# Modulation parts in four pieces, two PE sums moved into blocks, and a gate vector made as rows

## The reference, cut to what matters

```python
mod = split(silu(c) @ ada_w + ada_b, 6)              # six vectors of 1024
a = rmsnorm(x, g_pre) * (1 + mod[1]) + mod[0]
y = short_gated_conv(a)                              # a @ w_in (1024x3072), conv of 3 taps, @ w_out
h = x + mod[2] * rmsnorm(y, g_post)                  # mod[2]: the first gate vector
f = square(relu((rmsnorm(h, g_pre_ff) * (1 + mod[4]) + mod[3]) @ mlp_w_in)) @ mlp_w_out
h = h + mod[5] * rmsnorm(f, g_post_ff)
```

## Time and profile before

| | us |
|---|---|
| median of 3 runs | 749.37 (749.32 to 749.52) |
| profiled execution | 749.81 |
| its span, first to last instruction | 747.8 |
| PE busy | 740.4 (99%) |
| PEld, DVE, ACT, POOL busy | 690.1, 551.4, 366.7, 12.2 |
| granted TensorE clock | 1.00 in the whole span |
| bytes read from HBM | 151 MB, mean 203 GB/s |

### The profile page before, as it was taken

The page is one execution under the profiler, slowest core; times in us unless marked ns, Lnnn a source line. Parts: engine busy times, 40 slices in busy tenths (PEclk is TensorE's granted clock), DMA queues, the critical chain, the costliest instruction groups (busy, mean ns, idle before and its releaser), DMA issues.

```text
span 747.8 us, 13266 instructions
## 1 busy us (share of the span) xinstructions
PE 740.4 (99%) x5368; PEld 690.1 (92%) x5368; DVE 551.4 (74%) x767; ACT 366.7 (49%) x455; POOL 12.2 (2%) x29
## 2 busy tenths in 40 slices
PE   8999999999999999999999999999999999999998
PEld 8889956999998888899979999999999999999998
DVE  4569888865556734499899967859879988887441
ACT  4145232745553333496555366585556655554330
POOL 0000000000000000020000011000000000000000
PEclk9999999999999999999999999999999999999999
DMA  9999997354566967536545342437554555443640
GB/s 312 349 368 360 393 351 298 125 215 169 176 205 209 341 194 252 169 128 226 174 166 185 105 160 99 137 128 261 187 204 142 198 202 191 151 146 121 208 136 29
DMA packets 53583, 152.70 MB, mean 204 GB/s; under 512 B 2912, under 2 KB 34016, under 8 KB 43296
## 3 DMA queue, kind: packets, MB, share of 16 engines
q1 hardware_dynamic: 52704, 149.43, 58.3%
q0 software_dynamic: 544, 1.84, 0.7%
q10 hardware_dynamic: 288, 0.76, 0.3%
HBM read 150.97 MB, written 1.05 MB: 203 GB/s over the span
## 4 chain that ended last, share of the span: by engine, by line
PE 84%; DVE 8%; SPq 3%; ACT 3%; issue 1%; DMA 1%; DVEq 0%; ACTq 0%
PE ps L1533 19%; PE ps L1534 19%; PE ps L1535 19%; PE ps L1712 4%; PE ps L1713 4%; PE ps L1711 4%; PE ps L1758 4%; DVE w_lo L934 3%; SPq L420 2%; DVE cacc L1307 2%; PE ps L1617 1%; ACT w_hi L561 1%; DMA raw<-in_ada 1%; PE ps L1882 1%; PE ps L1880 1%
## 5 line engine op out<-in xcount | busy, mean ns | idle before, releaser
L934 DVE TENSOR_TENSOR w_lo<-raw,w_hi 128x2048 fp32r<-128x2048 f32 (+2 forms) x116 | 246.0, 2124 | 83.1 <-ACT w_hi L561 83.1
L1533 PE MATMUL ps<-a_hi,w_hi 128*128 128x256 f32 x1024 | 290.2, 283 | 0.0
L1534 PE MATMUL ps<-a_lo,w_hi 128*128 128x256 f32 x1024 | 289.0, 282 | 0.0
L1535 PE MATMUL ps<-a_hi,w_lo 128*128 128x256 f32 x1024 | 288.6, 282 | 0.0
L561 ACT ACTIVATE w_hi<-raw 128x2048 fp32r<-128x2048 f32 (+2 forms) x116 | 205.8, 1778 | 97.8 <-PE ps L1713 43.9
L1533 PEld LDWEIGHTS ps<-a_hi,w_hi 128*128 128x128 f32 x1024 | 193.2, 189 | 1.2 <-issue 0.7
L1534 PEld LDWEIGHTS ps<-a_lo,w_hi 128*128 128x128 f32 x1024 | 192.5, 188 | 0.6 <-issue 0.5
L1535 PEld LDWEIGHTS ps<-a_hi,w_lo 128*128 128x128 f32 x1024 | 192.8, 188 | 0.0
L1533 PE MATMUL ps<-up_hi,w_hi 128*128 128x256 f32 x192 | 54.7, 285 | 0.0
L1534 PE MATMUL ps<-up_lo,w_hi 128*128 128x256 f32 x192 | 54.2, 282 | 0.0
L1535 PE MATMUL ps<-up_hi,w_lo 128*128 128x256 f32 x192 | 53.8, 280 | 0.0
(11 more groups left out here) (289 smaller groups left out, 949.3 us busy)
## 6 DMA issues: line engine op xcount, KB each, us to landing
raw<-in_w_z_in SPq DMA_DIRECT2D x26, 1024.0 KB, 4.8
raw<-in_w_up SPq DMA_DIRECT2D x22, 1024.0 KB, 4.8
raw<-in_w_mlp_in SPq DMA_DIRECT2D x16, 1024.0 KB, 5.0
raw<-in_w_mlp_out SPq DMA_DIRECT2D x16, 1024.0 KB, 6.1
raw<-in_w_down SPq DMA_DIRECT2D x16, 704.0 KB, 4.1
raw<-in_ada_half SPq DMA_DIRECT2D x8, 1024.0 KB, 6.8
raw<-in_ada SPq DMA_DIRECT2D x8, 1024.0 KB, 6.5
raw<-in_w_sc_in SPq DMA_DIRECT2D x8, 768.0 KB, 7.1
```

The lines of the kernel that those rows point to most:

```text
L934: e.tensor_tensor(w_lo[:, slot, 0:words], raw[:, unit_slot, 0:words], w_hi[:, slot, 0:words].bitcast(f32), SUB).then_inc(raw_used, 1)
L1533: e.matmul(dst, w_hi[:, slot, cols], hi, start=start, stop=False, skip_group_check=skip)
L1534: e.matmul(dst, w_hi[:, slot, cols], lo, start=False, stop=False, skip_group_check=skip)
L1535: return e.matmul(dst, w_lo[:, slot, cols], hi, start=False, stop=stop, skip_group_check=skip)
```

## The change

1. Each part is loaded in four pieces in place of three, all of 256 KB (`PIECES`). DVE and PE wait for them piece by piece; the order of their operations stays. `COLUMNS_BEHIND` for tile 1 goes from product 9 to product 8.
2. `mod_sums` for vector 2, `widen`, the bias sum and weight product in columns, and the two copies are gone. In their place PE makes two products of 512 columns with a stationary matrix of ones (`row_sums`), which leave the sum over partitions as a row on every partition. They stand in group (0, 1) behind its fourth product. DVE adds the bias row and multiplies by the weight row (`gain_rows`), and does so between the low parts of mlp_in blocks 0 and 1.
3. The two rows come over DRAM: once PE is through the split keys, POOL writes columns of `par` (norm weight, bias) as rows to `param_rows` and reads each back on all partitions into `y`.
4. The sum for the convolution's mean moves behind the second product of the next block, the folded sum of ln2 behind the first k of the first up block.

```diff
-PIECES = [(0, 0, 4), (1, 0, 2), (1, 2, 4)]
+PIECES = [(0, 0, 2), (0, 2, 4), (1, 0, 2), (1, 2, 4)]
...
+            e.wait_ge(w_used, USED)
+            e.wait_ge(act_hi, DT)
+            e.wait_ge(act_lo, DT)
+            for n, (name, first) in enumerate((("gains", 8), ("ada_b", 16))):
+                e.dma_start(param_rows[n:n + 1, :].rearrange("o (i p) -> p (o i)", p=P), pcol(name, first, DT),
+                            allow_slow_non_contiguous=True).then_inc(row_out, 16)
+            e.wait_ge(row_out, 32)
+            for n in range(2):
+                e.dma_start(flat(y[:, 4 * n:4 * n + 4, :]), param_rows[n:n + 1, :].broadcast_to([P, D])).then_inc(row_in, 16)
...
-            def gain_evict(dst, n):
-
+            def gain_rows(dst):
+
+                e.wait_ge(row_in, 32)
+                start = ch.n
                 for h in range(2):
-                    e.wait_ge(gain_wide, 2 * n + h + 1)
-                    e.tensor_copy(dst[:, h * 512:(h + 1) * 512], ps[:, 6 + h, :]).then_inc(gain_in, 1)
-                e.wait_ge(gain_in, 2 * n + 2)
+                    cols = slice(h * 512, (h + 1) * 512)
+                    e.wait_ge(gain_wide, h + 1)
+                    ch.mark(e.tensor_tensor(dst[:, cols], ps[:, 6 + h, :], flat(y[:, 4 + 2 * h:6 + 2 * h, :]), ADD))
+                for h in range(2):
+                    cols = slice(h * 512, (h + 1) * 512)
+                    ch.wait(start + h + 1)
+                    e.tensor_tensor(dst[:, cols], dst[:, cols], flat(y[:, 2 * h:2 * h + 2, :]), MUL).then_inc(gain_in, 1)
...
             ahead_at(g0)
+            gain_rows(gain_b)
             ahead_at(g0 + 1)
-            mods(0, 2)
-            e.tensor_tensor(gain_post[:, :], mod[:, 16:24], pcol("gains", 8, 8), MUL).then_inc(gain_cols, 1)
...
-            COLUMNS_BEHIND = {1: 9, 3: 8, 5: 6}
+            COLUMNS_BEHIND = {1: 8, 3: 8, 5: 6}
...
+            def row_sums(acc):
+
+                for h in range(2):
+                    e.matmul(ps[:, 6 + h, :], ones[:, :], acc[:, h * 512:(h + 1) * 512], start=True, stop=True).then_inc(gain_wide, 1)
...
-                        if (c, h) == (1, 0) and k == 4:
-                            widen(gain_post, 0)
+                        if (c, h) == (0, 1) and k == 4:
+                            e.wait_ge(raw_used, ring_unit("half", 7) + 1)
+                            row_sums(ada_acc[:, 0, :])
...
-                    if (c, h) == (0, 1):
-                        e.wait_ge(raw_used, ring_unit("half", 7) + 1)
-                        mod_sums(2, ada_acc[:, 0, :], MISC)
...
+                    elif s == CV_MEAN_STEP + 1:
+                        pair_block(raw_unit(g0 + s) + 1, g0 + s, f % 2, a_hi, a_lo, lambda t: conv_mean() if t == 1 else None)
...
+                    if k == 1:
+                        folded_pairs_sum()
```

More of the change, by code:

```diff
@@ L255, in build_program @@
         x_new = sem("x_new")
-        part_in = [[sem(f"part_in{i}_{h}") for h in range(3)] for i in range(PARTS)]
+        part_in = [[sem(f"part_in{i}_{h}") for h in range(len(PIECES))] for i in range(PARTS)]
         key_in = [[sem(f"key_in{q}_{h}") for h in range(2)] for q in range(4)]
@@ L275, in build_program @@
         gain_wide = sem("gain_wide")
+        row_out = sem("row_out")
+        row_in = sem("row_in")
+        param_rows = nc.dram_tensor("param_rows", (2, D), f32).ap()
         gain_row_out = sem("gain_row_out")
@@ L430, in pair_parts @@
                     for u in both:
-                        for piece in range(3):
+                        for piece in range(len(PIECES)):
                             part_piece(u, piece)
                 else:
-                    for piece in range(3):
+                    for piece in range(len(PIECES)):
                         for u in both:
@@ L509, in _ @@
             constant(e.memset(sc_cv[:, :, :], 0.0), 4)
-            e.wait_ge(gain_cols, 2)
+            e.wait_ge(w_used, USED)
[7 more added lines that the diff above has]
+                e.dma_start(flat(y[:, 4 * n:4 * n + 4, :]), param_rows[n:n + 1, :].broadcast_to([P, D])).then_inc(row_in, 16)
+            e.wait_ge(gain_cols, 1)
             e.dma_start(gain_row.rearrange("o (i p) -> p (o i)", p=P), gain_post_ff[:, :],
@@ L1080, in token_chain @@
                 behind()
-            MOD_SUMMED, MOD_BANK = (1, 2, 3, 4), (MISC, 0, 1, MISC)
+            MOD_BANK = (0, 1, MISC)
             def mods(number, vector):
-                e.wait_ge(mod_ps, MOD_SUMMED[number])
+                e.wait_ge(mod_ps, number + 1)
                 cols = slice(8 * vector, 8 * vector + 8)
@@ L1215, in _ @@
             ahead_at(g0)
+            gain_rows(gain_b)
             ahead_at(g0 + 1)
-            mods(0, 2)
-            e.tensor_tensor(gain_post[:, :], mod[:, 16:24], pcol("gains", 8, 8), MUL).then_inc(gain_cols, 1)
             for i in range(2):
                 ada_unit(ring_unit("shift", i), 2 * i, ada_acc[:, 2, :])
-            gain_evict(gain_b, 0)
+            e.wait_ge(gain_in, 2)
             e.wait_ge(x_tok_in, 2)
@@ L1229, in scale_columns @@
             def scale_columns():
-                mods(1, 4)
+                mods(0, 4)
                 ch.mark(e.scalar_tensor_tensor(gain_pre_ff[:, :], mod[:, 32:40], 1.0, pcol("gains", 16, 8), ADD, MUL))
-            token_chain("post", 1, gain_b, x_tok, x_t, scale_columns, lambda: mods(2, 3))
+            token_chain("post", 1, gain_b, x_tok, x_t, scale_columns, lambda: mods(1, 3))
             ch.wait()
@@ L1253, in _ @@
                 if j == 7:
-                    mods(3, 5)
+                    mods(2, 5)
                     e.tensor_tensor(gain_post_ff[:, :], mod[:, 40:48], pcol("gains", 24, 8), MUL).then_inc(gain_cols, 1)
@@ L1633, in _ @@
             shift_column(0, 0)
+            shift_column(0, 1)
             e.wait_ge(x_r, 1)
             shift_column(1, 0)
-            shift_column(0, 1)
+            shift_column(1, 1)
             shift_column(0, 2)
+            shift_column(0, 3)
             scale_column(0)
-            shift_column(1, 1)
             shift_column(1, 2)
+            shift_column(1, 3)
             scale_column(1)
@@ L1941, in spatial_gating, with conv_mean @@
                 mm.then_inc(sg_done, 1)
+            def conv_mean():
+                e.wait_ge(cv_folded, 3)
+                e.wait_ge(rstd_ready, STATN["cv"])
+                e.matmul(ps[:, STAT, 0:T], ones[:, :], sq[:, 0, 0:T], start=True, stop=True).then_inc(cv_mean, 1)
             for s, kind in enumerate(Z_ORDER):
@@ L1982, in _ @@
                         scores(p)
[L1983 to L1986, removed]
                 if s == CV_VAR_STEP:
@@ L2011, in _, with folded_pairs_sum @@
                 pair_block(raw_unit(g0 + j) + 1, g0 + j, MIX_BANK[j], a_hi, a_lo)
-            e.wait_ge(folded_sum, 1)
-            e.wait_ge(rstd_ready, STATN["ln2"])
-            e.matmul(ps[:, STAT, 0:T], ones[:, :], up_p[:, 0, :], start=True, stop=False)
             g0 = FIRST["up"]
             n = N_BLOCKS["up"]
+            def folded_pairs_sum():
+                e.wait_ge(folded_sum, 1)
+                e.wait_ge(rstd_ready, STATN["ln2"])
+                e.matmul(ps[:, STAT, 0:T], ones[:, :], up_p[:, 0, :], start=True, stop=False, skip_group_check=True)
             def last_pair_sum():
@@ L2022, in last_pair_sum @@
                 for h in range(2):
-                    mm = e.matmul(ps[:, STAT, 0:T], ones[:, :], sq[:, 1, h * T:(h + 1) * T], start=False, stop=h == 1)
+                    mm = e.matmul(ps[:, STAT, 0:T], ones[:, :], sq[:, 1, h * T:(h + 1) * T], start=False, stop=h == 1, skip_group_check=True)
                 mm.then_inc(sq_used, 1)
@@ L2028, in unscaled_block @@
                 e.wait_ge(free["up"], 1)
+                e.wait_ge(x_new, 6)
                 e.wait_ge(raw_used, raw_unit(g0) + 1)
                 for k in range(DT):
+                    if k == 1:
+                        folded_pairs_sum()
                     if k == 2:
```

2 lines of the change are left out of this document (removed).

## The result

The changed kernel took 755.17 us in the median of 4 runs (753.97 to 755.82), the kernel before 749.38 beside it; the ratio is 1.0074, with an interval of 1.0062 to 1.0087. The forecast was 761, and so the direction is right and the size is not: 5.8 us came where 11.6 were expected. The profiled execution of the changed kernel took 755.82 us, the slowest of the four; its span is 753.9 against 747.8.

What follows compares the result with a forecast made beforehand. PE, busy 740.4 of 747.8 us, was taken as the bound, with the early load stream close to full. Sum: 749.4 + 14.5 (wait) - 1.84 (gate sums) - 1.08 (moved sums) = 761.0 us; range 751 to 766.5.

Steps and rivals of the forecast that it cites:

- Two writes one after the other: 2 x 7.4 = 14.8 us in which the stream stands.: At about 65 us, POOL's two element-wise row writes each hold SP's load stream 7.4 us, one after the other.
- The wait of PE: Half unit 1 late by 16.1 us, less 0.84 free at VectorE and 0.8 slack at PE: PE waits 14.5 us.
- About 3 us before block 5: Part of PE's forecast wait: about 3 us before block 5, whose load is caught in the hold.
- The clock, "up to 2 us more": If five products behind PE's longest wait ran at half speed, up to 2 us more; left open.
- The broadcasts, 2.6 us less 1.3 of idle: Reading both rows back adds 1 MB to the stream, 2.6 us at 400 GB/s; 1.3 us fits slack at 70 to 75.
- any small transfer: The hold's upper bound: a write's 12.9 us less 3.5 us that any small transfer takes, 9.4 per write.
- The gate sums, 1.84: PE drops 3.56 us of mod sums and widening products for two products of 1.72 us: 1.84 us less, no wait.
- Two sums in blocks, 1.08: Moving the convolution mean (0.43 us) and folded sum (0.65 us) into blocks covers PE's waits: gain 1.08 us (0.5 to 1.1).
- Quarters, 0.43: Loading parts in quarters lets pair 2's column sums go one product earlier on PE: gain 0.43 us (0 to 1.4).
- (a): Rival: the writes hold nothing and only PE's shorter queue remains, 746.0 us (745.4 to 747.5); chance 0.17.
- (b): Rival: one hold instead of two, or the stream keeps a share of turns, 753.6 us (750 to 756); chance 0.15.
- The round-robin rule of the Trainium skill: An engine alternates between its queues packet by packet; if held for 4-byte pieces, half the turns are the stream's.

Runs made afterwards that it cites:

- experiment 3: The kernel before with only the two element-wise writes and the waits around them added, nothing read back: 756.21 us, ratio 1.0085.
- experiment 6: The changed kernel with six unread products of 512 columns in front of PE's longest wait: 752.20 us, ratio 1.0034 to the kernel before.
- Experiment 1: The changed kernel without the two element-wise writes, both rows read back from an input instead: 745.01 us, ratio 0.994 to the kernel before.
- experiment 4: As Experiment 1, plus two 4 KB writes to DRAM in pieces of 512 bytes: 745.45 us, ratio 0.9947 to the kernel before.
- experiment 7: The kernel before with only the parts in quarters and the column sums one product earlier: 749.16 us, ratio 0.9995.
- experiment 5: The changed kernel with each row written as 128 pieces of 32 bytes, VectorE reading with a stride of eight: 746.68 us, ratio 0.9964 to the kernel before.
- experiment 2: The changed kernel with one element-wise write, the bias row read from an input: 753.48 us, ratio 1.006 to the kernel before.

## Why the prediction was right in direction and wrong in size

- **"Two writes one after the other: 2 x 7.4 = 14.8 us in which the stream stands."** This step failed. One write costs the stream 6.7 us, near the 7.4 taken from the earlier trace rows; but two cost 9.2, and 7.7 in experiment 3. They were issued 1 us apart and their packets went through together. The price per write was right, the multiplication wasn't; nothing in the trace of before showed two writes at once, and the sum should have carried both cases with like chances. Half unit 1 came 9.5 us late (92.75 for 83.24), not 16.1.
- **The wait of PE.** From 9.5 the same deductions (0.84 and 0.8) give 7.9 us; the gaps sum to 7.82. This step held, also in experiment 3: 5.6 less 0.84 and 0.8 is 4.0, and PE's gap is 3.9. "About 3 us before block 5" didn't happen: its load landed at 67.28, just before the stream stopped. Nor did PE wait before the row sums; all of it stands before the sc_out products.
- **The clock, "up to 2 us more" and left out of the sum.** It cost 2.7 us by the rows and 2.3 by experiment 6. The products named, the five behind the longest wait, are the ones that slowed down, but the bound of 2 was worked out wrong: five products of 0.858 us at half speed are 4.3 us more, and the 2.7 measured lie within that. With a wait of 3.7 us (experiment 3) it fell as well, to 0.50 from 105 to 110. Left out of the sum, it hides part of the error of the first step: without the fall of the clock the measured time would have lain some 2.7 us further from the forecast. That is luck.
- **The broadcasts, 2.6 us less 1.3 of idle.** Experiment 1 has them and nothing else new in this stretch of the stream: half unit 1 was 0.9 us late, and PE did not wait. Right. The 3.5 us of "any small transfer" in the upper bound was low: experiment 4's 4 KB writes took 5.2 and 6.1.
- **The gate sums, 1.84.** 1.85 by the rows; the slack before the row sums held without the writes. Right.
- **Two sums in blocks, 1.08.** The folded sum gave its 0.65. The mean gave nothing in the end. The working asked what is late next for the folded sum, and not for the mean: the variance sum 7 us behind it stood with no slack, on a chain of VectorE and ScalarE that the move did not touch.
- **Quarters, 0.43.** PE reached sc_out 0.15 us sooner in the changed kernel's profile and 0.35 in experiment 7's, whose median says 0.4: about right, and too small to be sure of. But the working took the wrong pair. The line of the diff moves the column sums behind tile 1, which are pair 1's (26.43 in the kernel before); those of pair 2, at 38.33 in the earlier trace rows, stay behind the same product. Pair 1's now stand before their data, and PE waits 1.7 us for them.
- **Not in the sum at all:** 1.8 us from the place of tensors in SBUF. The only sign of it in the change is the deleted `gain_post`.
- **Rivals.** (a) is what experiment 1 shows once the writes are gone, 745.0 for a worked-out 746.0: the place of the tensors, less the mean and perhaps part of the quarters. (b), one hold in place of two, with 753.6, was nearest to what happened; it had 0.15. That it came so near is in part chance: its terms were a hold of 7.4 and no clock, measured were 9.2 and 2.7, and 1.8 came back.

The account by terms: 7.82 + 2.72 - 1.85 - 0.15 - 0.65 - 1.8 = 6.1 us, the difference of the spans.

The round-robin rule of the Trainium skill (DMA: Bandwidth & Descriptors, "Queues, rings and completion order"), by which the stream should have kept half of the turns, isn't borne out as a share of bytes: 36 GB/s from 70 to 75 us. As a rule of turns it is neither shown nor refuted: the writes' packets were nearly all through by 68.4, and SP's own packets were slow. The Trainium skill's rule that a non-contiguous last dimension becomes one descriptor per element (same page, "Rules for kernel authors") fits experiment 5 against the changed kernel: what was paid for was the cut into pieces of 4 bytes, not the bytes.

## What to carry to other kernels

Price a DMA by how it is cut and not by its bytes alone: a 4 KB write of single floats cost the stream as much as 2.7 MB of loads, the same bytes in pieces of 32 bytes or more next to nothing; such a write belongs where nobody waits for loads, or its layout is to be changed. When a stretch of PE's queue is moved under cover, follow the freed result to its next consumer, and when PE must wait for some microseconds, add to the wait what the slower clock costs behind it, or fill the wait with products. Before a gain or loss of 0.2% is put down to an edit, look whether the edit moved tensors in memory.

## What the runs showed of the hardware that was not expected

- Element-wise writes hold another queue's transfers, and two at once hold little longer than one: 6.7 us against 7.7 to 9.2 us of a full stream. The hold begins some 6 us after the issue, and the stream needs 5 to 7 us to recover. The writes' own packets take 0.08 us each; it is single packets of the other queue that take up to 7.9 us.
- The start of tensors in SBUF changes PE's pace in products of 256 columns with f32r operands by up to 1.9% (0.3533 to 0.3600 us for three), 1.8 us in this kernel.
- Six unread products in a wait of 6 us kept the clock at 1.00 and saved 2.3 us behind it. Waits of 3.7, 5.3 and 6.0 us (experiments 3 and 2, the changed kernel) were each followed by a clock of about 0.50, which cost 2.6 to 2.8 us.
- VectorE took 1.0 us for 128x512 with one f32 operand at a stride of 32 bytes, 0.64 with all contiguous. The Trainium skill (SBUF — State Buffer, "Door 1: The DMA port swizzle") speaks of lines of 16 bytes in SBUF, beyond which a stride costs; this trace agrees in direction, 1.0 against 0.64 us.
